# A second norm written chunk by chunk, and the gather that loads its rows as stationaries

## The chip, the cores and the metric

One core of a Trainium2 chip runs the whole step in one launch. The metric is the device time of that launch in microseconds (us): the median of the runs, 1483.82 us before. The engines are TensorE (PE, with its weight loads shown apart as PEld), VectorE (DVE), ScalarE (ACT), GpSimd (POOL) and SyncE (SP), which issues most of the DMAs.

## The reference, cut to what matters

One layer of a streaming encoder on 384 tokens (256 of a prompt, 8 x 16 of samples) with a model width of 1024, all in float32: a projection, a pooling branch and sparse attention, an output projection, and then

```
h2 = rmsnorm(x, norm2_g)                        # x / rms(x) * g, per token
logits = h2 @ w_router + b_router               # 32 experts, the best 4 of each token
for each expert e, on its tokens:
    gu = xe @ w_gate_up[e] + b_gate_up[e]       # 1024 -> 2 x 1024
    a  = min(g, 7) * sigmoid(1.702 g) * (clip(u, -7, 7) + 1)
    y  = a @ w_down[e] + b_down[e]              # 1024 -> 1024
x = x + sum over the 4 experts of gate * y
```

The weights of the 32 experts are 32 x (8 + 4) MB, and each is read once from HBM.

## The kernel before, in words

The tokens are NT = 3 tiles of 128 rows. The width of 1024 is worked on in KC = 8 chunks of 128 for the contraction. Chunk c holds the columns c, c + 8, c + 16, ... (index q * 8 + c), since the weights are loaded with eight neighbouring rows per partition.

**Head.** The projection, attention and the output projection come first. Line 1348 is the output projection, and line 914 adds it to x. The second norm (lines 906 to 909) follows on DVE: `h2[:, t, :]` is x times the reciprocal root times the row `g2row`, three instructions of 1024 elements, one per token tile. PE transposes h2 (lines 1357 and 1361, 24 transposes of 128 x 128) for the router (line 1368). In a transpose h2 is the stationary operand and the identity is the moving one. DVE then works out the selection and the rank of each token in its expert.

**Experts.** The experts go in pairs, two at a time, 64 slots each. DVE writes a 0/1 matrix `pick` (tokens x 128 slots, line 987) for a pair. The gather on PE (line 1404) multiplies it with h2, so that the chosen tokens land transposed in PSUM: 8 chunks times 3 tiles, `h2[:, t, c::KC]` as the stationary and `pick` as the moving operand. A float32 product is two loads and two matmuls in the trace, so a gather is 48 instructions of each kind. ACT (line 672) and DVE (line 993) copy the result to xT. Then come the gate and up products (line 1418, eight units of 1 MB of weights per expert), the transposes back (line 1471), the activation on DVE and ACT, the down products (line 1429, four units per expert), and the rows are added back by a third product (line 1438) and DVE (line 1018).

PE's order is written out by hand: `gather(1)` and the eight gate and up units of expert 0, then 15 turns of a loop, each with two experts and the gather of the next pair between the gate and up units and the down units of its first expert, then a last turn without a gather. So there are 16 gathers, of which 15 are in the loop.

**The weights' queue.** SP issues the expert weights as 384 DMAs of 1 MB in the order in which PE takes them, into 12 slots. The first 12 are loaded during the head. Each later one waits until PE has used the unit 12 places earlier (`unit_used`, line 394), and PE waits for each unit's landing (`slot_wait`, line 1410).

Of the kernel before, what the change touches and what calls it, by code (L numbers as in the profile page):

```python
# [22 lines left out]
ALU = mybir.AluOpType  # L23
# [3 lines left out]
P = 128  # L27
D = 1024
KC = D // P
SEQ, DEC_B, DEC_S, PAST = 256, 8, 16, 128  # L30
NT = (SEQ + DEC_B * DEC_S) // P
# [98 lines left out]
def build(nc, I, O):  # L130
    keep = ExitStack()
    with keep:
        def sem(name):
            return keep.enter_context(nc.semaphore(name))
# [5 lines left out]
        def fixed(name, shape, dt=F32):  # L140
            n = int(np.prod(shape[1:])) * 4
            t = nc.alloc_sbuf_tensor_at(name, shape, dt, offset=cursor[0])
            cursor[0] += (n + 31) // 32 * 32
            return t

        ring = fixed("ring", [P, RING, UCOL])
        x = fixed("x", [P, NT, D])
# [9 lines left out]
        def at(name, kib, shape, dt=F32):  # L157
            off = region + int(kib * 1024)
            assert off + int(np.prod(shape[1:])) * 4 <= nc.sbuf_usable_end, (name, off)
            return nc.alloc_sbuf_tensor_at(name, shape, dt, offset=off)  # L160
# [50 lines left out]
        mix_a = at("mix_a", 92, [P, 512])  # L211
        mixT = at("mixT", 120, [P, KC, TOK])

        h2 = at("h2", 64, [P, NT, D])
        sq2 = at("sq2", 76, [P, D])
        h2T = at("h2T", 114, [P, KC, TOK])
        rt = at("rt", 126, [P, 8, NT * E])
# [17 lines left out]
        g2row = at("g2row", 60, [P, D])  # L235
        eps = small[:, 0:1]
        ssx = small[:, 1:4]
        rsx = small[:, 4:7]
# [8 lines left out]
        bank = [keep.enter_context(nc.psum_tensor(f"bank{i}", [P, 512], F32)) for i in range(8)]  # L247
        scratch = nc.dram_tensor("bias_rows", [H, NREL], F32)

        ident = cst[:, C_ID:C_ID + P]  # L250
        ustrict = cst[:, C_US:C_US + P]

        def bc(t, off, dims, parts=P, p0=0):

            row = int(np.prod(t.shape[1:]))
            return bass.AP(t, off + p0 * row, [[row, parts]] + [list(d) for d in dims])
# [24 lines left out]
        sumsq2, rms2, h2_ready, h2_turned, h2t_ready, route_done = (sem(s) for s in ("sumsq2", "rms2", "h2_ready", "h2_turned", "h2t_ready", "route_done"))  # L281
# [21 lines left out]
        V, A, T, G = nc.vector, nc.scalar, nc.tensor, nc.gpsimd  # L303
# [14 lines left out]
        def half_head(h):  # L318
            return h // 2, 64 * (h % 2)
# [402 lines left out]
        def _(dve):  # L722
            count = [0]

            def step(ins):

                count[0] += 1
                ins.then_inc(vchain, 1)
                dve.wait_ge(vchain, count[0])
# [53 lines left out]
            def ones_like(ap):  # L783
                n = ap.shape[1]
                return bc(small, 95, [(0, n)])
# [110 lines left out]
            for k, m in enumerate(MIXED):  # L896
                t, n = divmod(m, 2)
# [6 lines left out]
            def second_norm(t):  # L904

                dve.wait_ge(rms2, t + 1)
                dve.wait_ge(x1_ready, 2 * (t + 1))
                step(V.reciprocal(rsx[:, t:t + 1], rsx[:, t:t + 1]))
                V.scalar_tensor_tensor(h2[:, t, :], x[:, t, :], rsx[:, t:t + 1], g2row[:], ALU.mult, ALU.mult).then_inc(h2_ready, 1)

            for m in range(2 * NT):
                t, n = divmod(m, 2)
# [3 lines left out]
                if m == 4:  # L916
                    dve.wait_ge(g2_in, 16)
                    second_norm(0)
                    second_norm(1)
            second_norm(2)  # L920
            dve.wait_ge(h2_ready, NT)
            for c in range(1, KC, 2):
# [14 lines left out]
            for t in range(NT):  # L937
                last = V.max(small[:, 8 + 8 * t:16 + 8 * t], lg[:, t * E:(t + 1) * E])
# [7 lines left out]
            for t in range(NT):  # L946
                c = slice(t * E, (t + 1) * E)
                last = V.tensor_tensor_scan(pre[:, c], ones_like(eq[:, c]), eq[:, c], 0.0, ALU.mult, ALU.add)
# [14 lines left out]
            for q in range(MAXPASS):  # L963
                last = V.tensor_scalar(rank_all[:, q, :, :], rt[:, 5, :].rearrange("p (t e) -> p e t", t=NT), -float(q * SLOTS),
                                       None, ALU.add)
# [40 lines left out]
            for u in range(2 * NT):  # L1006
                t, h = divmod(u, 2)
# [59 lines left out]
        def _(pe):  # L1067
# [3 lines left out]
            for c in range(KC):  # L1071
                for t in range(NT):
                    last = T.transpose(bank[c][:, t * P:(t + 1) * P], xn[:, t, c::KC], ident)
# [7 lines left out]
            def turn_twice(b, col, rows):  # L1081

                for r in (0, 64):
                    last = T.matmul(b[r:r + 64, col:col + P], rows, ident, start=True, stop=True)
                return last
# [21 lines left out]
            for b in range(4):  # L1107
                last = turn_twice(bank[7], b * P, ikc[:, b, :])
            last.then_inc(pe_small, 1)
            pe.wait_ge(small_out, 1)  # L1110
            for b in range(4):
                last = turn_twice(bank[6], b * P, ikc[:, 4 + b, :])
# [5 lines left out]
            for t in range(2):  # L1118
                for c in range(2):
                    last = T.transpose(bank[7][:, (2 * t + c) * P:(2 * t + c + 1) * P], zi[:, t, c * P:(c + 1) * P], ident)  # L1120
# [3 lines left out]
            for t in range(2):  # L1124
                last = turn_twice(bank[6], (2 + t) * P, zi[:, t, 256:320])
# [35 lines left out]
            for m in range(5):  # L1161
                if m >= 2:
                    pe.wait_ge(flip_out, m - 1)
                if m < 4:
                    last = T.matmul(bank[6 + m % 2][:, :], flip[:, 0:P], biasR[:, 2 * m:2 * m + 2, :].rearrange("p h k -> p (h k)"),
                                    start=True, stop=True)
                else:
                    last = T.matmul(bank[6][:, 0:PAST + DEC_S], flip[:, P:2 * P], bS0[:], start=True, stop=True)
# [20 lines left out]
            for m in range(8):  # L1189
                if m >= 2:  # L1190
                    pe.wait_ge(turned_out, m - 1)
                for t in range(NT):
                    last = T.transpose(bank[6 + m % 2][:, t * P:(t + 1) * P], zqk[:, t, m * P:(m + 1) * P], ident)
# [32 lines left out]
            for t in range(2):  # L1226
# [5 lines left out]
                for h in range(H):  # L1232
                    c, r = half_head(h)
                    b = bank[h % 2 + 2 * (c // hpb)]
                    col = (c % hpb) * nk
                    last = T.matmul(b[:, col:col + nk], qT[r:r + 64, c, t * P:(t + 1) * P], kT[r:r + 64, c, 0:nk],
                                    start=True, stop=True)
# [4 lines left out]
                for h in range(H):  # L1242
                    c, r = half_head(h)
                    for kc in range(nkc):
                        last = T.matmul(bank[0][r:r + 64, c * P:(c + 1) * P], zv[:, kc, h * HD:(h + 1) * HD],
                                        pT[:, h * nkc + kc, :], start=(kc == 0), stop=(kc == nkc - 1))
# [5 lines left out]
            for r in range(2):  # L1252
                unit_wait(pe, kc_u + r)
                for m in range(4):
                    if r:
                        pe.wait_ge(ks_out, 4)
                    for c in range(PAIRS):
                        last = T.transpose(bank[4 + m][:, c * P:(c + 1) * P],
                                           ring[:, (kc_u + r) % RING, m * 512 + c * P:m * 512 + (c + 1) * P], ident)
# [3 lines left out]
                for m in range(4):  # L1263
# [4 lines left out]
                    for c in range(PAIRS):  # L1268
                        T.matmul(out[:, o:o + P], qblk[:, m, c, :], kTs[:, m, c, :], start=False, stop=False)  # L1269
                        last = T.matmul(out[:, o + P:o + 256], qblk[:, m, c, :], kT[:, c, 2 * P:], start=False,  # L1270
                                        stop=(c == PAIRS - 1))
# [12 lines left out]
            def branch(m, src, u0, b, c):  # L1284

                t, n = divmod(m, 2)
                o = (c % 2) * D + 512 * n
                return T.matmul(bank[b][:, :], src[:, c, t * P:(t + 1) * P], ring[:, (u0 + c // 2) % RING, o:o + 512],  # L1288
                                start=(c == 0), stop=(c == 3))
# [4 lines left out]
            for b in range(DEC_B):  # L1294
                for half in range(2):
                    for c in (2 * half, 2 * half + 1):
# [3 lines left out]
                        last = T.matmul(out, zv[:, 2, c * P:(c + 1) * P], pT[:, 2 * b + 1, 32 * c:32 * c + 32], start=False, stop=True)  # L1300
                    if b >= 2:
                        m, c = dense[2 * (b - 2) + half]
# [16 lines left out]
            for n, m in enumerate(MIXED):  # L1319
# [7 lines left out]
                for c in range(4):  # L1327
                    last = branch(m, attT, wba_u, 2 * (m % 4) + 1, c)
# [4 lines left out]
            for m in range(2 * NT):  # L1333
                t, hf = divmod(m, 2)
                pe.wait_ge(mix_ready, 2 * NT)
                for q in range(4):
                    last = T.transpose(bank[m][:, q * P:(q + 1) * P], mixed[:, t, 4 * hf + q::KC], ident)
# [3 lines left out]
            for m in range(2 * NT):  # L1341
                t, n = divmod(m, 2)
# [3 lines left out]
                for c in range(KC):  # L1346
                    o = (c % 2) * D + 512 * n
                    last = T.matmul(bank[6 + m % 2][:, :], mixT[:, c, t * P:(t + 1) * P],  # L1348
                                    ring[:, (wo_u + c // 2) % RING, o:o + 512], start=(c == 0), stop=(c == KC - 1))
# [4 lines left out]
            pe.wait_ge(h2_ready, 2)  # L1354
            for c in range(6):
                for t in range(2):
                    T.transpose(bank[c][:, t * P:(t + 1) * P], h2[:, t, c::KC], ident)
            pe.wait_ge(h2_ready, NT)
            for c in range(KC):
                for t in range(2 if c < 6 else 0, NT):  # L1360
                    last = T.transpose(bank[c][:, t * P:(t + 1) * P], h2[:, t, c::KC], ident)
                last.then_inc(h2_turned, 1)
            pe.wait_ge(h2t_ready, KC // 2)
            pe.wait_ge(ht_ready_v, KC)
# [1 line left out]
            for t in range(NT):  # L1366
                for c in range(KC):
                    last = T.matmul(bank[0][:, t * E:(t + 1) * E], h2T[:, c, t * P:(t + 1) * P], wr[:, c, :],  # L1368
                                    start=(c == 0), stop=(c == KC - 1))
            last.then_inc(route_done, 1)  # L1370

            for hf in range(2):
# [3 lines left out]
                for c in range(KC):  # L1376
                    last = T.transpose(bank[1][:, c * E:(c + 1) * E], bgn[:, c::KC], cst[0:E, C_ID:C_ID + E])
# [9 lines left out]
            for t in range(NT):  # L1387
                last = T.matmul(bank[0][:, 128:128 + E], ones, sel[:, t * E:(t + 1) * E], start=(t == 0), stop=(t == NT - 1))
# [3 lines left out]
            for t in range(NT):  # L1392
                last = T.transpose(bank[5][0:E, t * P:(t + 1) * P], rt[:, 1, t * E:(t + 1) * E], ident)
# [5 lines left out]
            def gather(pairs):  # L1399

                pe.wait_ge(pick_ready, pairs)
                for c in range(KC):
                    for t in range(NT):
                        last = T.matmul(bank[2 + c // 4][:, (c % 4) * P:(c % 4 + 1) * P], h2[:, t, c::KC],  # L1404
                                        pick[:, t, :, :].rearrange("p a s -> p (a s)"), start=(t == 0), stop=(t == NT - 1))
                last.then_inc(gathered, 1)

# [36 lines left out]
            for u in range(KC):  # L1444
                if u < 2 * NT:

                    t, h = divmod(u, 2)
# [81 lines left out]
```

## Time and profile before

| what | us |
|---|---|
| median of 3 runs | 1483.82 (1481.07 to 1484.92) |
| the profiled execution, its own time | 1482.67 |
| its span, first to last instruction | 1480.8 |
| PE matmul busy in the span | 1409.2 (95%) |
| PE weight loads busy | 677.5 (46%) |
| DVE busy | 425.2 (29%) |
| ACT busy | 189.9 (13%) |

HBM read in the span is 439.27 MB. The page names an operand without its buffer number, so h2 reads as `h`; behind the arrow the moving operand stands first and the stationary second (`bank<-pick,h`). A load and its matmul have the same line. Busy times of PE overlap, since a matmul starts before the one ahead of it has ended: how fast a stretch goes is read from the start of one group to the start of the next.

### The profile page before, as it was taken

What the parts mean: (1) busy time and instruction counts of PE and PEld (TensorE: products, weight loads), DVE (VectorE), ACT (ScalarE), POOL (GpSimd) and SP (SyncE); (2) the same over time, 40 slices, a digit from 0 to 9 for tenths busy, and PEclk for the clock granted to TensorE, in tenths of its full rate; (3) what the DMA queues carried; (4) which work ended last, traced back from release to release, by engine and by line L of the source; (5) the groups of instructions that cost most, each with busy time, mean ns of one, the idle gap of its engine ahead of it and who ended that gap; (6) DMA issues with size and microseconds to landing.
All of it is one profiled execution on the core that took longest, in us unless ns stands there. A gap on an engine that the chain in (4) does not pass through costs nothing.

```text
span 1480.8 us, 15864 instructions
## 1 busy us (share of the span) xinstructions
PE 1409.2 (95%) x6011; PEld 677.5 (46%) x6011; DVE 425.2 (29%) x762; ACT 189.9 (13%) x360; POOL 33.2 (2%) x36
## 2 busy tenths in 40 slices
PE   5999996899989999999999999999999999999996
PEld 3445454664472543535355353544535354353532
DVE  1164013312223222242322324222232322224233
ACT  3121222300110010110101101010110101011000
POOL 4000003000000000000000000000000000000000
PEclk9999997899969999999999999999999999999998
DMA  8221430314429899999999999999999999999991
GB/s 299 94 77 58 145 114 0 121 57 162 165 96 347 322 422 376 380 418 367 423 377 420 376 367 422 372 423 372 390 407 374 424 366 422 375 378 417 374 422 50
DMA packets 73332, 443.14 MB, mean 299 GB/s; under 512 B 7971, under 2 KB 9787, under 8 KB 23646
## 3 DMA queue, kind: packets, MB, share of 16 engines
q1 hardware_dynamic: 68992, 434.94, 72.6%
q10 hardware_dynamic: 3054, 4.90, 1.0%
q0 software_dynamic: 1264, 2.99, 0.7%
q8 instruction: 16, 0.26, 0.1%
q14 instruction: 6, 0.05, 0.0%
HBM read 439.27 MB, written 3.53 MB: 299 GB/s over the span
## 4 chain that ended last, share of the span: by engine, by line
PE 79%; DVE 2%; DMA 1%; ACT 1%; issue 0%; DVEq 0%; SPq 0%; POOL 0%; PEldq 0%
PE bank L1418 31%; PE bank L1429 15%; PE bank L1404 13%; PE bank L1438 7%; PE bank L1288 3%; PE bank L1348 3%; PE bank L1471 2%; PE bank L1484 1%; DMA wpool<-in_w_pool 1%; PE bank L1368 1%; PE bank L1300 1%; PE bank L1299 0%; PE bank L1270 0%; PE bank L1269 0%; DMA ring<-in_w_out 0%; ACT logit L593 0%
## 5 line engine op out<-in xcount | busy, mean ns | idle before, releaser
L1418 PE MATMUL bank<-ring,xT 128*64 128x512 f32 x2048 | 474.9, 600 | 0.0
L1418 PEld LDWEIGHTS bank<-ring,xT 128*64 128x64 f32 x2048 | 132.7, 136 | 284.5 <-issue 280.0
L1429 PE MATMUL bank<-ring,aT 128*64 128x512 f32 x1024 | 226.9, 596 | 0.0
L1404 PEld LDWEIGHTS bank<-pick,h 128*128 128x128 f32 x768 | 184.1, 335 | 15.8 <-issue 12.2
L1404 PE MATMUL bank<-pick,h 128*128 128x128 f32 x768 | 187.1, 405 | 3.2 <-DVE pick L987 3.2
L1018 DVE TENSOR_TENSOR x<-x,bank 128x512 f32<-128x512 f32 x198 | 127.2, 684 | 128.5 <-PE bank L1438 128.5
L1098 PE MATMUL bank<-ring,hT 128*128 128x512 f32 (+1 forms) x384 | 159.1, 574 | 1.0 <-DMA ring<-in_w_in 0.7
L1429 PEld LDWEIGHTS bank<-ring,aT 128*64 128x64 f32 x1024 | 72.4, 137 | 139.9 <-issue 138.1
L1438 PE MATMUL bank<-yS,back 64*128 64x512 f32 x396 | 112.9, 647 | 8.4 <-DVE x L1018 7.6
L1098 PEld LDWEIGHTS bank<-ring,hT 128*128 128x128 f32 x384 | 72.3, 190 | 83.9 <-issue 79.8
L1031 DVE TENSOR_TENSOR gz<-bank,bguT 128x512 f32<-128x512 f32 x64 | 41.2, 686 | 218.9 <-PE bank L1471 218.9
L998 DVE COPY gus<-bank 128x512 f32<-128x512 f32 x32 | 22.1, 692 | 194.9 <-PE bank L1418 194.9
L1438 PEld LDWEIGHTS bank<-yS,back 64*128 64x128 f32 x396 | 30.0, 186 | 88.4 <-DVE x L1018 61.4
L993 DVE COPY xT<-bank 128x512 f32<-128x512 f32 x16 | 11.1, 693 | 174.6 <-PE bank L1404 174.6
L688 ACT ACTIVATE back<-bank 128x384 f32<-128x384 f32 x32 | 15.7, 491 | 343.4 <-PE bank L1484 343.4
L693 ACT ACTIVATE yS<-bank 128x512 f32<-128x512 f32 x32 | 19.1, 597 | 204.2 <-PE bank L1429 204.2
L1471 PEld LDWEIGHTS bank<-cst,gus 128*128 128x128 f32 x256 | 31.1, 194 | 27.0 <-issue 25.2
L1348 PE MATMUL bank<-ring,mixT 128*128 128x512 f32 x96 | 41.4, 593 | 1.1 <-DMA ring<-in_w_out 1.1
L677 ACT ACTIVATE gus<-bank 128x512 f32<-128x512 f32 x32 | 19.1, 598 | 167.2 <-PE bank L1418 167.2
L1471 PE MATMUL bank<-cst,gus 128*128 128x128 f32 x256 | 37.2, 288 | 1.0 <-DVE gus L998 1.0
L672 ACT ACTIVATE xT<-bank 128x512 f32<-128x512 f32 x16 | 9.6, 598 | 179.7 <-PE bank L1404 179.7
L1348 PEld LDWEIGHTS bank<-ring,mixT 128*128 128x128 f32 x96 | 18.2, 190 | 24.0 <-issue 24.0
(247 smaller groups left out, 779.9 us busy)
## 6 DMA issues: line engine op xcount, KB each, us to landing
ring<-in_w_gate_up SPq DMA_DIRECT2D x256, 1024.0 KB, 9.2
ring<-in_w_down SPq DMA_DIRECT2D x128, 1024.0 KB, 9.3
ring<-in_w_in SPq DMA_DIRECT2D x16, 1024.0 KB, 8.0
ring<-in_w_out SPq DMA_DIRECT2D x4, 1024.0 KB, 5.9
ring<-in_cache_k SPq DMA_DIRECT2D x2, 1024.0 KB, 6.8
ring<-in_cache_v SPq DMA_DIRECT2D x2, 1024.0 KB, 6.7
ring<-in_w_branch_pool SPq DMA_DIRECT2D x2, 1024.0 KB, 6.9
ring<-in_w_branch_attn SPq DMA_DIRECT2D x2, 1024.0 KB, 11.3
```

Source lines behind the costliest of these rows:

```text
L677: A.activation(gus[:, 0:512], bank[0][:, :], ACT.Copy).then_inc(gu_out_a, 1)
L998: V.tensor_copy(gus[:, 512:FF], bank[1][:, :]).then_inc(gu_out_v, 1)
L1018: V.tensor_tensor(x[:, t, 512 * h:512 * h + 512], x[:, t, 512 * h:512 * h + 512], bank[6 + h][:, :], ALU.add).then_inc(y_added, 1)
L1031: V.tensor_tensor(gz[:, 4 * b:4 * b + 4, :, :], bank[2 + b][:, :].rearrange("p (c h s) -> p c h s", c=4, h=2), bc(bguT, bias + 4 * b, [(1, ...
L1098: last = T.matmul(bank[3 * (m % 2) + t][:, 0:w], hT[:, c, t * P:(t + 1) * P], ring[:, u % RING, (c % 4) * w:(c % 4 + 1) * w], start=(c == ...
L1288: return T.matmul(bank[b][:, :], src[:, c, t * P:(t + 1) * P], ring[:, (u0 + c // 2) % RING, o:o + 512], start=(c == 0), stop=(c == 3))
L1348: last = T.matmul(bank[6 + m % 2][:, :], mixT[:, c, t * P:(t + 1) * P], ring[:, (wo_u + c // 2) % RING, o:o + 512], start=(c == 0), stop=( ...
L1404: last = T.matmul(bank[2 + c // 4][:, (c % 4) * P:(c % 4 + 1) * P], h2[:, t, c::KC], pick[:, t, :, :].rearrange("p a s -> p (a s)"), start ...
L1418: last = T.matmul(bank[j][64 * r:64 * r + 64, :], xT[:, w, SLOTS * a:SLOTS * a + SLOTS], src[:, FF * r + 512 * j:FF * r + 512 * j + 512], ...
L1429: last = T.matmul(bank[4][64 * r:64 * r + 64, :], aT[:, c, :], src[:, o:o + 512], start=(c == 0), stop=(c == KC - 1))
L1438: last = T.matmul(bank[6 + h][:, :], back[64 * h:64 * h + 64, t, :], yS[64 * h:64 * h + 64, :], start=True, stop=True)
L1471: last = T.transpose(bank[2 + c // 4][:, (c % 4) * P:(c % 4 + 1) * P], gus[:, c::KC], ident)
```

## The change

The tile h2 gets the same bytes in another order. It is now `[128, 3, 8, 128]`: for each token the 128 elements of chunk 0 stand together, then those of chunk 1, and so on. The norm writes it so by reading x and the gain row through a view that steps by 8 elements (32 bytes) within a chunk. The transposes and the gather then take a chunk as 128 neighbouring elements. Number, shape and order of the instructions on all engines are the same as before, as are the waits.

```diff
-        h2 = at("h2", 64, [P, NT, D])
+        h2 = at("h2", 64, [P, NT, KC, P])
...
+        def by_chunk(ap):
+            return ap.rearrange("p (q c) -> p c q", c=KC)
...
-                V.scalar_tensor_tensor(h2[:, t, :], x[:, t, :], rsx[:, t:t + 1], g2row[:], ALU.mult, ALU.mult).then_inc(h2_ready, 1)
+                V.scalar_tensor_tensor(h2[:, t, :, :], by_chunk(x[:, t, :]), rsx[:, t:t + 1], by_chunk(g2row[:]), ALU.mult, ALU.mult).then_inc(h2_ready, 1)
...
-                    T.transpose(bank[c][:, t * P:(t + 1) * P], h2[:, t, c::KC], ident)
+                    T.transpose(bank[c][:, t * P:(t + 1) * P], h2[:, t, c, :], ident)
...
-                    last = T.transpose(bank[c][:, t * P:(t + 1) * P], h2[:, t, c::KC], ident)
+                    last = T.transpose(bank[c][:, t * P:(t + 1) * P], h2[:, t, c, :], ident)
...
-                        last = T.matmul(bank[2 + c // 4][:, (c % 4) * P:(c % 4 + 1) * P], h2[:, t, c::KC],
+                        last = T.matmul(bank[2 + c // 4][:, (c % 4) * P:(c % 4 + 1) * P], h2[:, t, c, :],
                                         pick[:, t, :, :].rearrange("p a s -> p (a s)"), start=(t == 0), stop=(t == NT - 1))
```

## Rows read from the trace of the kernel before

**Rows 1.** The chain that ended last, by line, from the page.
```profile
PE bank L1418 31%; PE bank L1429 15%; PE bank L1404 13%; PE bank L1438 7%; PE bank L1288 3%; PE bank L1348 3%; PE bank L1471 2%; PE bank L1484 1%; DMA wpool<-in_w_pool 1%; PE bank L1368 1%; PE bank L1300 1%; PE bank L1299 0%; PE bank L1270 0%; PE bank L1269 0%; DMA ring<-in_w_out 0%; ACT logit L593 0%
```
**Rows 2.** PE's waits from 442 to 1450 us: total, times, longest.
```profile
PE bank L1471 <- DVE gus L998: 1.0, 1, 1.0
```
**Rows 3.** PE in order of time, two gathers: start, length, line, operands.
```profile
483.41 11.69 PE L1404 MATMUL bank<-pick,h 128*128 128x128 f32 x48
495.03 7.09 PE L1429 MATMUL bank<-ring,aT 128*64 128x512 f32 x32
...
547.39 11.69 PE L1404 MATMUL bank<-pick,h 128*128 128x128 f32 x48
```
**Rows 4.** Weight loads by line and shape: busy us, mean ns, idle before.
```profile
L1404 PEld LDWEIGHTS bank<-pick,h 128*128 128x128 f32 x768 | 184.1, 335 | 15.8 <-issue 12.2 <-DVE pick L987 3.6
...
L1269 PEld LDWEIGHTS bank<-kTs,qblk 128*128 128x128 f32 x64 | 10.3, 192 | 0.4
...
L1258 PEld LDWEIGHTS bank<-cst,ring 128*128 128x128 f32 x32 | 3.5, 141 | 1.4 <-issue 1.4
...
L1361 PEld LDWEIGHTS bank<-cst,h 128*128 128x128 f32 x12 | 1.4, 194 | 2.3 <-DVE h L909 2.3
```
**Rows 5.** PE in order of time, first 16 attention products of lines 1269, 1270.
```profile
255.54 0.38 PE L1269 MATMUL bank<-kTs,qblk 128*128 128x128 f32 x2
...
257.33 0.60 PE L1267 MATMUL bank<-neg,rep 128*128 128x256 f32 x2
```
**Rows 6.** The same view, 16 products of lines 1299 and 1300.
```profile
292.06 0.61 PE L1299 MATMUL bank<-pT,ring 128*128 128x32 f32 x2 [1.96 <-DMA wpool<-in_w_pool]
...
295.47 1.20 PE L1309 MATMUL bank<-ext,wpool 128*128 128x256 f32 x2
```
**Rows 7.** Stretches: us, busy by engine, granted clock, DMA share, GB/s.
```profile
255.50:257.30 1.80, 1.80 (x17) 1.77 (x17) 0.00 (x0) 0.00 (x0) 0.00 (x0) 1.00 0.00 0
292.00:295.40 3.40, 3.34 (x16) 3.37 (x17) 0.00 (x0) 1.70 (x4) 0.00 (x0) 0.50 1.03 410
...
430.60:434.60 4.00, 4.00 (x17) 4.00 (x17) 0.82 (x2) 0.00 (x0) 0.00 (x0) 0.50 0.00 0
434.60:438.60 4.00, 4.00 (x19) 4.00 (x18) 0.00 (x0) 0.00 (x0) 0.00 (x0) 0.85 0.00 0
...
446.00:490.00 44.00, 43.04 (x180) 17.66 (x179) 13.53 (x22) 3.80 (x6) 0.00 (x0) 1.00 0.99 375
490.00:496.00 6.00, 6.00 (x28) 5.31 (x29) 0.69 (x1) 0.60 (x1) 0.00 (x0) 1.00 0.12 51
505.00:552.00 47.00, 47.00 (x211) 17.89 (x208) 16.27 (x28) 5.22 (x9) 0.00 (x0) 1.00 1.01 421
...
1337.00:1384.00 47.00, 47.00 (x211) 18.10 (x207) 16.13 (x27) 4.97 (x9) 0.00 (x0) 1.00 1.01 422
```
**Rows 8.** PE in order of time, the first gather and the first unit.
```profile
430.55 11.75 PE L1404 MATMUL bank<-pick,h 128*128 128x128 f32 x48 [3.16 <-DVE pick L987]
...
443.28 1.94 PE L1418 MATMUL bank<-ring,xT 128*64 128x512 f32 x8
```
**Rows 9.** DVE: the third norm; then two lines' ns, min/median/max, and shapes.
```profile
405.63 1.28 DVE L909 SCALAR_TENSOR_TENSOR h<-x,small,g2row 128x1024 f32<-128x1024 f32 x1
...
L964 DVE TENSOR_SCALAR rank_all<-rt x6: 204/206/217, 426.7 to 427.4; 128x96 f32<-128x96 f32 x6
...
L792 DVE TENSOR_SCALAR neg<-is_gt x3: 226/293/293, 79.3 to 136.7; 128x256 f32<-128x256 f32 x2, 128x128 f32<-128x128 f32 x1
```
**Rows 10.** The page's DMA issues: count, KB each, us to landing.
```profile
ring<-in_w_gate_up SPq DMA_DIRECT2D x256, 1024.0 KB, 9.2
ring<-in_w_down SPq DMA_DIRECT2D x128, 1024.0 KB, 9.3
```
**Rows 11.** PE in order of time, the last turn.
```profile
1449.97 1.16 PE L1471 MATMUL bank<-cst,gus 128*128 128x128 f32 x8
...
1461.22 8.06 PE L1429 MATMUL bank<-ring,aT 128*64 128x512 f32 x32
```

## The prediction

> **What bounds the kernel now.** I read the chain of waits first. PE's expert products hold most of it, and the gather alone (line 1404) 13% [rows 1]. The list of waits says whether the weights are late: from 442 to 1450 us PE waited once, 1.0 us, for DVE, and never for a weight [rows 2]. So the loop runs at PE's pace, and what a gather gives back counts until something else is late. PE in order of time gives the sizes: the gather takes from 483.41 to 495.03, 11.62 us, and the next starts at 547.39, 63.98 us after the first [rows 3]. The stretches show the queue that stands behind PE: in 14 stretches of 47 us, one in each of 14 loop turns, the weights came at 420 to 423 GB/s with a DMA share of 1.01, the first at 421 and the last at 422. Around the end of the second gather the queue idled, 51 GB/s from 490 to 496, because all slots were full [rows 7]. A unit of 1.0486 MB at 422 GB/s is 2.485 us. A loop turn takes 24 of them, 59.6 us, so the weights have only 4.3 us of slack in 63.98.
>
> **The gather in the loop.** 48 instructions in 11.62 us are 242 ns from start to start. Is it the stationary's step? A gather's load lasts 335 ns; that of line 1269, whose stationary is contiguous and whose shape is the same, 192. Line 1361, a transpose of the stepped h2, loads in 194, and line 1258, a transpose of a contiguous tile, in 141 [rows 4]. In both kinds the stepped operand costs more. The first gather is a second witness: its first stretch ran at a granted clock of 0.50, its end at full clock [rows 7], and yet it took 11.7 us like the others [rows 3, 8]. PE's clock does not set its pace; the read of the stationary can.
>
> The pace without the step is read from lines 1269 and 1270: same type, 128 x 128 stationary, 128 moving columns. 16 instructions start from 255.54 to 257.33, 112 ns each, at a granted clock of 1.00 [rows 5, 7]. That makes a gather 48 x 0.112 = 5.4 us, a saving of 6.2 us, and 15 times that is 94. From the other side: if loads hid behind nothing, each at 192 ns, a gather would take 9.2 us and save 2.4. If the pace has another cause, it saves nothing. I take 112, since it is the measured pace of the same shape.
>
> The skill's rule beside these rows: the Trainium skill, "SBUF — State Buffer", section "Door 1: The DMA port swizzle", says that SBUF is read in lines of 16 bytes and that each access that crosses to a new line pays, so that float32 steps for free only up to 4 elements. The step here is 8. The loads of 335 against 192 ns agree.
>
> **The first gather** ran at half clock from 430.55; the clock of 0.85 over 434.6 to 438.6 puts the rise at 435.8. At half clock a contiguous stationary goes at 213 ns: 16 instructions from 292.06 to 295.47, clock 0.50 [rows 6, 7]. If the rise stays where it was, 5.25 us hold 24.6 instructions, and the other 23.4 take 2.6 us: 7.9 against 11.7, so 3.8 us saved. With the clock low to the end it would take 10.2 (1.5 saved), at full clock all through 5.4 (6.3 saved).
>
> **The second norm.** Three instructions of 1.28 us, of which the third stands on the path [rows 9]; the others run beside the output projection. They now read two operands in steps of 32 bytes. Line 964 reads 96 elements in steps of 128 bytes in 206 ns; line 792, the same operation on contiguous data, takes 226 for 128 and 293 for 256 [rows 9]. That is 0.52 ns per element and extrapolates to 209 for 96: no penalty shows, so I take 0. Were a stepped read as dear as in the gather, 242 / 128 = 1.9 ns per element, and the two operands read one after the other, an instruction would take 3.9 us; all three on the path would add 7.8 us. A gain is not excluded, but I see no row for one.
>
> The rule above speaks against this edit: by it the norm pays what the gather is spared. The 206 ns do not show that, and the sum by it stays within the 7.8 us just bounded.
>
> **The transposes** of lines 1357 and 1361 lose some 53 ns of load each, 12 of them on the path [rows 4]. DVE's and ACT's copies follow them one for one and are slower, so I count 0; if all of it showed, 0.6 us.
>
> **What is late next.** PE alone: 94 + 3.8 = 98 us off, a span of 1480.8 - 98 = 1383, and 63.98 - 6.2 = 57.7 us per turn. The weights need 59.6. PE starts the loop with 12 loaded units, falls behind by 1.9 us a turn of that lead, and from about the middle waits for landings. The end by the weights: the first loop unit is released when the first eight products of line 1418 end, 445.2 [rows 8]; 3.8 us earlier now, 441.4. The first 16 units after that took until 490.5 (375 GB/s over 44 us is 16.5 MB, the stretch behind it 0.3 [rows 7]), 45.3 us, because PE releases them slowly there beside the down-bias products. That stays, and the second gather is now over before the slots fill, so the queue does not idle again. There are 256 + 128 units [rows 10], of which 12 are preloaded and 16 just counted; the last four arrive during the last turn's own work of 11.3 us, between 1449.97 and 1461.22 [rows 11], and do not bind. That leaves 384 - 12 - 16 - 4 = 352 units of 2.485 = 874.7 us: 441.4 + 45.3 + 874.7 = 1361.4. PE takes that unit in 1.8 us, and what follows it (from 1449.97 to the span's end) took 30.8: span 1394. This is later than PE's 1383, so it binds. The saving is 87 us, not 98.
>
> The profiled execution took 1482.67, 1.9 us over its span, and the median of the runs is 1.15 above that. 1394 + 3 gives **1397 us**.
>
> **Rivals.**
> Half the gain: the loads are not hidden at 192 ns each, a gather of 9.2 us; 15 x 2.4 + 1.5 = 38 us, 1446. Paces between lie between; at 145 ns the loop is PE's, a gather of 7.0, and the time is 1412. Lines 1269 and 1270 speak against it, since their loads last 192 and still go every 112.
>
> The weights are no bound: PE's 1383 + 3, so 1386. That would need over 436 GB/s (25.17 MB in 57.7 us); no stretch of 47 us shows over 423. The page cited above, in section "SBUF: two separate sides", gives 436 GB/s as the DMA ceiling and 432 as measured; by 432 the time would be 1386 to 1387 too. The traces bear that out little, 422 being steady.
>
> It doesn't do what it says: 242 ns come from another operand; 1484. Against it stand rows 4; `pick` and the PSUM target are contiguous.
>
> Slower: the waits for landings take PE's clock away. The first gather, after 3.16 us without work, ran at a clock of 0.50, where an instruction costs 213 instead of 112 ns [rows 6 to 8]. Each us of PE work then costs nearly one more. It decides when over 6.3 of the 57.7 us in a turn run at half clock; at a fifth of them a turn takes 69.2 us and the time is 1386 + 15 x 11.5 = 1558. For it: PE will wait. Against: 1.9 us of waiting per turn, split over several units, under a us each, and PE is busy 97% of the turn.
>
> **How the numbers follow.** Forecast 0.72, own range 1388 to 1406: the rate of 420 to 423 is ±4, the norm up to +7.8, the first gather ±2.4. No bound by the weights 0.08, half the gain or so 0.13, no effect 0.04, slower 0.03. The range 1382 to 1418 holds the first two and the near part of the third. This kernel's runs differ by some 0.3%, about 4 us, which is what a measurement can tell; by that faster is 0.93, no change 0.04, slower 0.03.
>
> **What would show it.** A gather of 5.4 us in PE's order; loads of line 1404 near 192 ns; from the middle of the loop waits of line 1418 and 1429 for DMA into the ring, with 422 GB/s and no idle stretch; turns of 57.7 us early and 59.6 late; line 909 still at 1.28. I am wrong if a gather stays above 7 us, if the loop's clock leaves 1.00, or if the rate of the weights is another once they bind.

## The result, and the profile after

The changed kernel takes 1407.7 us (median of 4 runs, 1405.8 to 1410.0) against 1482.9 before (by now the median of 4 runs): a ratio of 0.949 with a 95% interval of 0.947 to 0.952. The forecast was 1397, its range 1382 to 1418. The profiled execution took 1405.8 us, with a span of 1404.0.

The new view reads like the old one: the page's chain by line, in which the lines named have moved by four (the gather is line 1408 now, the expert products 1422 and 1433).

```profile
PE bank L1422 27%; PE bank L1433 13%; DMA ring<-in_w_gate_up 9%; PE bank L1408 6%; PE bank L1442 6%; DMA ring<-in_w_down 4%; PE bank L1352 3%; PE bank L1292 3%; PE bank L1475 2%; PE bank L1488 1%; DMA wpool<-in_w_pool 1%; PE bank L1304 1%; PE bank L1372 1%; PE bank L1274 1%; PE bank L1273 1%
```

The gather fell from 13% to 6%, and 13% of the chain are now DMAs of expert weights, which the list before does not have [rows 1]. The list of PE's waits from 442 to 1373 us (total, times, longest) names them, where only the last of these rows stood before [rows 2]:

```profile
PE bank L1433 <- DMA ring<-in_w_down: 6.1, 14, 0.7
PE bank L1422 <- DMA ring<-in_w_gate_up: 1.3, 4, 0.6
PE bank L1475 <- DVE gus L1002: 1.0, 1, 1.0
```

PE in order of time (start, length, line), at two early and two late gathers:

```profile
482.63 5.62 PE L1408 MATMUL bank<-pick,h 128*128 128x128 f32 x48
488.18 7.09 PE L1433 MATMUL bank<-ring,aT 128*64 128x512 f32 x32
...
540.53 5.62 PE L1408 MATMUL bank<-pick,h 128*128 128x128 f32 x48
...
1242.48 5.62 PE L1408 MATMUL bank<-pick,h 128*128 128x128 f32 x48
...
1302.20 5.62 PE L1408 MATMUL bank<-pick,h 128*128 128x128 f32 x48
```

A gather takes 488.18 - 482.63 = 5.55 us in place of 11.62 [rows 3], 116 ns per instruction. The early turn is 57.9 us long, the late one 59.7. All turns from the second gather to the one at 1003.7 take 57.9, the five after it 59.6 to 59.7. The weight loads (busy us, mean ns, idle before), of the gather and of the two groups of transposes of h2:

```profile
L1408 PEld LDWEIGHTS bank<-pick,h 128*128 128x128 f32 x768 | 88.7, 195 | 15.8 <-issue 12.2 <-DVE pick L991 3.6
...
L1365 PEld LDWEIGHTS bank<-cst,h 128*128 128x128 f32 x12 | 2.4, 223 | 3.2 <-DVE h L913 3.2
...
L1361 PEld LDWEIGHTS bank<-cst,h 128*128 128x128 f32 x12 | 1.3, 140 | 0.9 <-issue 0.9
```

The gather's 195 and line 1361's 140 are close to the 192 and 141 ns of the contiguous tiles [rows 4]. Line 1361 here was line 1357 before, with a median load of 193 ns. Line 1361 of [rows 4] is line 1365 now, and it shows no gain, 223 ns for 194. But the granted clock was 0.52 over its 3.5 us and 1.00 before, so these two cannot be compared. The stretches show the weights' queue (columns as in [rows 7]):

```profile
434.10:438.10 4.00, 3.96 (x19) 3.96 (x20) 0.86 (x2) 0.00 (x0) 0.00 (x0) 0.53 0.00 0
...
444.40:490.00 45.60, 44.64 (x213) 17.44 (x213) 14.20 (x23) 4.40 (x7) 0.00 (x0) 1.00 0.97 366
490.00:540.00 50.00, 50.00 (x230) 16.46 (x228) 17.62 (x30) 5.52 (x9) 0.00 (x0) 1.00 0.99 405
540.00:598.00 58.00, 58.00 (x290) 22.59 (x286) 19.00 (x32) 6.71 (x11) 0.00 (x0) 1.00 1.01 422
1200.00:1260.00 60.00, 59.08 (x290) 22.52 (x290) 18.99 (x32) 6.71 (x11) 0.00 (x0) 1.00 1.01 421
444.40:1371.00 926.60, 917.20 (x4469) 349.51 (x4467) 297.98 (x501) 103.10 (x170) 0.00 (x0) 1.00 1.01 418
```

From 540 to 1368 us every stretch of 6 us shows 415 to 429 GB/s; an idle one like that of 51 GB/s before [rows 7] is gone. The units stay in the queue for longer: from issue to landing a gate and up unit now takes 21.3 us in place of 9.2 [rows 10].

```profile
ring<-in_w_gate_up SPq DMA_DIRECT2D x256, 1024.0 KB, 21.3
```

DVE's third norm, and PE's first gather, first unit and last turn, in order of time:

```profile
408.45 2.05 DVE L913 SCALAR_TENSOR_TENSOR h<-x,small,g2row 128x1024 f32<-128x1024 f32 x1
```
```profile
434.14 7.38 PE L1408 MATMUL bank<-pick,h 128*128 128x128 f32 x48 [3.15 <-DVE pick L991]
441.45 1.12 PE L1454 MATMUL bank<-bdn,gT 32*128 32x512 f32 x2
442.50 1.94 PE L1422 MATMUL bank<-ring,xT 128*64 128x512 f32 x8
...
1371.12 1.94 PE L1433 MATMUL bank<-ring,aT 128*64 128x512 f32 x8 [0.54 <-DMA ring<-in_w_down]
1372.99 1.16 PE L1475 MATMUL bank<-cst,gus 128*128 128x128 f32 x8
...
1384.03 8.42 PE L1433 MATMUL bank<-ring,aT 128*64 128x512 f32 x32
```

The norm is dearer, 2.05 us for 1.28 [rows 9]. The first gather takes 7.3 us for 11.7 [rows 8]. The products of line 1433 at 1371.12 wait for their landing, as do those just before them.

### The profile page after: what moved, and what is told of

Read it like the earlier page. It is cut to its first block, busy times and chain, and to the rows that moved or that the text cites. A ratio compares the mean times of both kernels' runs of the same rounds, so it can differ in the third digit from the quotient of the medians.

```text
span 1404.0 us, 15864 instructions
## 1 busy us (share of the span) xinstructions
PE 1321.5 (94%) x6011; PEld 578.8 (41%) x6011; DVE 427.5 (30%) x762; ACT 189.5 (13%) x360; POOL 33.2 (2%) x36
## 4 chain that ended last, share of the span: by engine, by line
PE 65%; DMA 14%; DVE 2%; ACT 1%; issue 1%; DVEq 0%; SPq 0%; POOL 0%; PEldq 0%
PE bank L1422 27%; PE bank L1433 13%; DMA ring<-in_w_gate_up 9%; PE bank L1408 6%; PE bank L1442 6%; DMA ring<-in_w_down 4%; PE bank L1352 3%; PE bank L1292 3%; PE bank L1475 2%; PE bank L1488 1%; DMA wpool<-in_w_pool 1%; PE bank L1304 1%; PE bank L1372 1%; PE bank L1274 1%; PE bank L1273 1%
## 5 line engine op out<-in xcount | busy, mean ns | idle before, releaser
L1433 PE MATMUL bank<-ring,aT 128*64 128x512 f32 x1024 | 230.7, 598 | 6.4 <-DMA ring<-in_w_down 6.1
L1408 PEld LDWEIGHTS bank<-pick,h 128*128 128x128 f32 x768 | 88.7, 195 | 15.8 <-issue 12.2
L1408 PE MATMUL bank<-pick,h 128*128 128x128 f32 x768 | 91.8, 280 | 3.2 <-DVE pick L991 3.2
L829 DVE SCALAR_TENSOR_TENSOR logit<-bank,logit 128x512 f32<-128x512 f32 x6 | 3.8, 683 | 74.4 <-PE bank L1240 74.3
## 6 DMA issues: line engine op xcount, KB each, us to landing
ring<-in_w_gate_up SPq DMA_DIRECT2D x256, 1024.0 KB, 21.3
```

What stands on the lines that cost most here:

```text
L1433: last = T.matmul(bank[4][64 * r:64 * r + 64, :], aT[:, c, :], src[:, o:o + 512], start=(c == 0), stop=(c == KC - 1))
```

## The experiments

Times are medians with the number of runs where there are several; spans are those of the profiled execution.

**1. The gather alone in steps again.**

```diff
-                        last = T.matmul(bank[2 + c // 4][:, (c % 4) * P:(c % 4 + 1) * P], h2[:, t, c, :],
+                        last = T.matmul(bank[2 + c // 4][:, (c % 4) * P:(c % 4 + 1) * P], by_step(t, c, KC),
```
(`by_step(t, off, step)` is the view of the tile's 1024 columns from `off` in steps of `step`.)

> The changed kernel with the norm and the transposes by chunk, but the gather alone reads its stationaries in steps of 8 elements again (it so takes other columns of h2 than the reference). Theory A, the step of the stationary sets the gather's pace: 242 ns per instruction again, 11.6 us per gather, turns of 64.0 us, no wait of PE for a weight in the loop, a time of 1481 to 1488, some 1 us of it the dearer norm. Rival B, the gain came from the transposes or from the new place of the data: the gather stays near 5.6 us and the time near 1408.

Measured: 1485.6 us, span 1483.8. PE in order of time:

```profile
486.34 11.69 PE L1412 MATMUL bank<-pick,h 128*128 128x128 f32 x48
497.96 5.37 PE L1437 MATMUL bank<-ring,aT 128*64 128x512 f32 x24
```

The gather takes 11.62 us again, all loop turns 64.0, and PE waits for no weight. The chunked norm and the contiguous transposes are still there, so the gather's read accounts for the gain, and rival B falls.

**2. Which step costs: chunk c of a gather in steps of c + 1.**

```diff
+                for t in range(NT):
+                    last = T.matmul(bank[2][:, 0 * P:1 * P], by_step(t, 0, 1), ...)
+                for t in range(NT):
+                    last = T.matmul(bank[2][:, 1 * P:2 * P], by_step(t, 0, 2), ...)
...
```

> The changed kernel, but chunk c of a gather reads its stationary in steps of c + 1 elements, 1 to 8, each chunk on a line of its own (so it takes other columns of h2 than the reference). Theory A, the load pays for each line of memory that it touches anew: no more than 112 to 120 ns per instruction at steps 1 and 2, rising to 242 at step 8, with the jump at one step between. Rival B, any step other than 1 costs the whole 242. Rival C, the price grows evenly with the step, some 19 ns per element. The Trainium skill, SBUF - State Buffer, Door 1: The DMA port swizzle, puts the jump between 4 and 5 elements (16 bytes); by it chunks 1 to 4 take 0.67 us each and chunks 5 to 8 1.45 us, 8.5 us for a gather, against 10.9 by rival B.

Measured: 1454.9 us. One gather in order of time, steps 1 to 8 from top to bottom, and the line behind it:

```profile
484.80 0.94 PE L1411 MATMUL bank<-pick,h 128*128 128x128 f32 x6
485.57 0.87 PE L1413 MATMUL bank<-pick,h 128*128 128x128 f32 x6
486.28 1.21 PE L1415 MATMUL bank<-pick,h 128*128 128x128 f32 x6
487.32 1.56 PE L1417 MATMUL bank<-pick,h 128*128 128x128 f32 x6
488.72 1.52 PE L1419 MATMUL bank<-pick,h 128*128 128x128 f32 x6
490.07 1.51 PE L1421 MATMUL bank<-pick,h 128*128 128x128 f32 x6
491.42 1.54 PE L1423 MATMUL bank<-pick,h 128*128 128x128 f32 x6
492.80 1.59 PE L1425 MATMUL bank<-pick,h 128*128 128x128 f32 x6
494.32 6.23 PE L1449 MATMUL bank<-ring,aT 128*64 128x512 f32 x28
```

From start to start, by six: 128, 118, 173, 233, 225, 225, 230 and 253 ns. A step of 2 is free, 3 is half way, and from 4 on the price is nearly flat. Theory A holds in kind, though step 1 took 128 ns for its 112 to 120 and the rise takes two steps and not one. Rivals B and C fall: step 2 costs nothing, and step 4 costs 233 ns where an even growth gives about 170.

The first gather of this run shows what the clock has to do with it. These are its steps 2 to 5; the granted clock was 0.50 up to the start of the last line:

```profile
434.18 1.49 PE L1413 MATMUL bank<-pick,h 128*128 128x128 f32 x6
435.46 1.49 PE L1415 MATMUL bank<-pick,h 128*128 128x128 f32 x6
436.74 1.59 PE L1417 MATMUL bank<-pick,h 128*128 128x128 f32 x6
438.12 1.42 PE L1419 MATMUL bank<-pick,h 128*128 128x128 f32 x6
```

Steps of 2 and 3 go at 213 ns here, the pace that a contiguous stationary showed at half clock with 32 moving columns [rows 6], and a step of 4 at 230. At half clock, then, a step of 4 costs 17 ns per instruction; at full clock it costs over 100.

The Trainium skill, "SBUF — State Buffer", section "Door 1: The DMA port swizzle", names 16-byte lines and two hits per line for full rate. The rows agree with that: a step of 2 leaves two float32 in 16 bytes, a step of 4 one. They contradict the same passage where it lets float32 step by 4 for free; by that a gather would have taken 8.5 us, and it took 494.32 - 484.80 = 9.5.

**3. The norm reads straight and writes in steps.**

```diff
-                V.scalar_tensor_tensor(h2[:, t, :, :], by_chunk(x[:, t, :]), ...
+                V.scalar_tensor_tensor(h2[:, t, :, :].rearrange("p c q -> p q c"), x[:, t, :].rearrange("p (q c) -> p q c", c=KC), ...
```

> The changed kernel, but the norm reads x and the gain row as they stand and writes in steps: each element goes 128 elements (512 bytes) behind the last. The result in h2 is the same. In the changed kernel the norm took 2.05 us where it took 1.28 before. Theory A, the two stepped reads cost the 0.77 us and a stepped write costs nothing: 1.28 us again, and the first gather starts 0.8 us earlier after the end of the last output product. Rival B, any step costs, or a step of 512 bytes costs more: 2.05 us or above. The time moves by at most 3 us either way, so only the trace tells.

Measured: 1407.7 us. The third norm:

```profile
405.75 1.96 DVE L913 SCALAR_TENSOR_TENSOR h<-x,small,g2row 128x1024 f32<-128x1024 f32 x1
```

Theory A falls in its second half: a stepped write costs 0.68 us (1.96 - 1.28) where two stepped reads cost 0.77 (2.05 - 1.28). Of rival B it holds that any step costs; 1.96 is just below its 2.05.

**4. The norm's three tiles in steps of 2, 4 and 8.**

```diff
+                c = (2, 4, 8)[t]
-                V.scalar_tensor_tensor(h2[:, t, :, :], by_chunk(x[:, t, :]), ...
+                V.scalar_tensor_tensor(h2[:, t, :, :]..., by_chunk(x[:, t, :], c), ...
```

> The changed kernel, but the norm of the first token tile reads in steps of 2 elements (8 bytes), that of the second in steps of 4 (16 bytes), and that of the third in steps of 8 as the change has it (so the columns of h2 stand in another order than the reference's in the first two). Theory E, VectorE's read behaves as the stationary's load did, whose pace was that of a contiguous one at a step of 2 and nearly the full price at 4: 1.28, then 2.05, then 2.05 us. Rival F, VectorE pays for any step: 2.05 us in all three. Rival G, it pays only beyond 16 bytes: 1.28, 1.28, 2.05.

Measured, DVE in order of time (1408.5 us):

```profile
399.17 1.29 DVE L914 SCALAR_TENSOR_TENSOR h<-x,small,g2row 128x1024 f32<-128x1024 f32 x1
...
400.56 2.08 DVE L914 SCALAR_TENSOR_TENSOR h<-x,small,g2row 128x1024 f32<-128x1024 f32 x1
...
407.67 2.05 DVE L914 SCALAR_TENSOR_TENSOR h<-x,small,g2row 128x1024 f32<-128x1024 f32 x1
```

Theory E holds within 0.03 us in all three numbers. VectorE's reads are free at a step of 2 and pay in full at 4, as the stationary's load does; a step of 3 was not run here.

**5. Half of each down unit's bytes, in the changed kernel.**

```diff
-                    sp.dma_start(slot_of(DEPTH + k), src).then_inc(slot_in[k % DEPTH], 16)
+                    cols = UCOL if w < KC else UCOL // 2
+                    sp.dma_start(slot_of(DEPTH + k)[:, 0:cols], src[:, 0:cols]).then_inc(slot_in[k % DEPTH], 16)
```

> The changed kernel, but in the loop and the last turn a unit of the down weights loads only half of its columns (the other half of the slot keeps older data). A turn then moves 21.0 MB in place of 25.2, 49.7 us at 422 GB/s, and PE's work is the same. Theory A, from the tenth turn on the weights' queue sets the time: no wait for a landing is left, all turns take 57.9 us, 5 x 1.8 us of the late turns and some 5.7 us of the last turn go, and the span is 1404 - 14.6 = 1389 (with 3 us for the head's clock). Rival C, the late turns are longer for another reason (clock, memory traffic at large): they stay at 59.7 and the span near 1404.

Measured: 1393.6 us, span 1391.8. PE's waits from 442 to 1370:

```profile
PE bank L1444 <- DVE x L1024: 4.9, 2, 3.4
PE bank L1477 <- DVE gus L1004: 1.0, 1, 1.0
```

Two late gathers, PE in order of time:

```profile
1236.67 5.62 PE L1410 MATMUL bank<-pick,h 128*128 128x128 f32 x48
...
1294.57 5.62 PE L1410 MATMUL bank<-pick,h 128*128 128x128 f32 x48
```

No wait for a landing is left, and all 14 gather-to-gather times of the loop are 57.9 us. The first unit started 1.3 us later than in the changed kernel (443.84 against 442.50), and the span is 12.2 us shorter; from the first unit on it is 13.5 us, where 14.6 were expected. So the waits for the weights' queue make the late turns longer. Of rival C, the clock was 1.00 in early and late turns alike. The halving cuts the traffic as well, but the traffic is no cause either: in the changed kernel it was 422 GB/s in an early turn of 57.9 us and 421 in a late one of 59.7.

**6. The same halving in the kernel before.**

> The kernel before, but in the loop and the last turn a unit of the down weights loads only half of its columns. Theory A, the weights were no bound there, and what PE does goes no faster beside less traffic: turns of 64.0 us, a span of 1478 to 1484. Rival D, the traffic itself slows PE or the loads of its stationaries: turns under 63.5 us and a span under 1475.

Measured: 1483.9 us, turns of 63.97 to 63.98. The stretch of one turn (columns as above):

```profile
484.60:548.60 64.00, 64.00 (x289) 28.67 (x287) 19.01 (x32) 6.71 (x11) 0.00 (x0) 1.00 0.86 318
```

At 318 GB/s in place of some 393 (24 units in 64.0 us) PE's turn is as long as before: this traffic does not slow it, and rival D falls.

**7. The bias products moved to the last turn, and the changed kernel again.** The six products with the down bias leave the first eight units; they come behind the last four gate and up units and the first two down units of the last turn.

```diff
-                    T.matmul(bank[6 + u % 2][:, :], gT[:, t, :], bdn[:, 512 * h:512 * h + 512],
-                             start=True, stop=True).then_inc(bd_done, 1)
...
+                        if final and a == 0 and w >= 4:
+                            bias_rows(n, w - 4)
```

> The changed kernel as it is, timed in five rounds on the chip on which the next one is timed. Theory A, the loop goes from 57.9 us per turn to 59.7 when the weights bind, as in the first trace: ratio to before 0.947 to 0.952. What differs between runs of it is the head, where the granted clock falls for some us at other places each time: the last product of the output projection should start up to 4 us earlier or later.

> The changed kernel, but the six products with the down bias, which stand between the first eight weight units (6.3 us of PE), move to the last turn, where PE waits some 0.5 us for each of its last units. Not one product fewer. Theory A, the weights' queue sets the end: PE gets 6.3 us further ahead early, the units are released and loaded sooner, and in the last turn the products fill waits that are there anyway; part of the 6.3 us comes out, some 3.5 us by a count with the releases, so a span some 3 to 5 us under that of the changed kernel, a ratio of the two of about 0.9975. Rival C, PE's own work sets the end: the work is only moved, and the time stays within 1 us.

DVE's six additions of these products move with them.

Measured, five runs each on the same chip: the changed kernel 1408.2 us (1404.9 to 1410.2; 0.949 of before, 0.947 to 0.952), the other 1404.4 (1402.8 to 1408.1; 0.947, 0.944 to 0.949). The medians differ by a ratio of 0.9974, as expected, but the runs and the intervals overlap, so the times do not tell the two apart. The changed kernel's second profile goes from turns of 57.9 to 59.7 us again, and its transposes behind the output projection start at 405.41, against 406.14 in the first, within the 4 us expected.

The spans miss what was expected, 3 to 5 us less: 1403.8 with the late bias, 1404.0 and 1403.1 in the two profiles of the changed kernel. The traces say where it went. Late bias, PE in order of time, and a stretch behind the last transposes (columns as in [rows 7]):

```profile
434.84 8.52 PE L1416 MATMUL bank<-pick,h 128*128 128x128 f32 x48 [3.15 <-DVE pick L991]
444.35 13.96 PE L1430 MATMUL bank<-ring,xT 128*64 128x512 f32 x64 [0.99 <-DVE xT L997]
...
1371.84 1.16 PE L1485 MATMUL bank<-cst,gus 128*128 128x128 f32 x8
...
1377.00:1381.00 4.00, 2.08 (x4) 0.50 (x4) 2.22 (x5) 0.00 (x0) 0.00 (x0) 0.50 0.00 0
```

From the end of the first gather to the last transposes it takes 928.5 us, against 931.5 in the changed kernel (1372.99 - 441.52), with the six products in both. 3.0 us came out (2.7 against the second profile), and rival C's exact balance does not fit. The first unit now waits 0.99 us for DVE's xT; that is within the 928.5, and the first bias product's 1.05 us stood there before. But this run's first gather ended 1.8 us later than in the first profile of the changed kernel, and the tail behind the last transposes took 32.0 us for 31.0: the granted clock was 0.50 from 1377 to 1381 us, where the changed kernel had 0.82 from 1378 to 1381. That leaves the 0.2 us between the spans of 1403.8 and 1404.0. Whether the whole launch is faster stays open.

## Why the prediction held, and where it was off

**The gather.** The pace of 112 ns per instruction was read from another line and came out as 116. 15 times (11.62 - 5.55) is 91 us, where 94 stood in the sum. That the gather did not follow PE's clock was the right witness: experiments 1 and 2 show the read of the stationary as the cause. Of the signs named, the gathers of the loop are under 7 us. The first one took 7.3, under the 7.9 of the sum.

**The weights.** The bound named as next is the one found, from the gather at 1003.7 us on, somewhat past the middle of the loop. PE's turns are 57.9 (57.7 forecast), the queue's 59.7 (59.6 forecast). Experiment 5 puts the price of this bound at 13.5 us from the first unit on (12.2 of the span, as its head was later); the forecast was 1394 - 1383 = 11.

**The 10 us between the spans of 1394 and 1404.0.** The median of 1407.7 is within the wide range but 1.7 us above the prediction's own one, 1388 to 1406. By the sum's own terms (the median stands 3.7 us above its profile's span, where 3 was added):

- The weights' term was 6.7 us short. From the first release at 444.4 to the unit at 1371.1 it took 926.7 us, and 45.3 + 874.7 = 920 were forecast. "The queue does not idle again" held, but full rate began a turn late: 405 GB/s over the 50 us from 490 cost 2 us. The rate behind it was 421 to 422, worth another 1 us or so on 352 units. And 418 GB/s over 926.6 us are 369.4 units, where 368 were counted. The stretch behind agrees: from 1371.1 to 1384 us 3.1 MB came, 2.9 units, where four were still to come by the sum. So bytes of later units had landed before the one that PE waited for, 1.1 to 1.4 units or some 3 us. That the deeper queue is the reason is argued and not shown.
- The head was 2.8 us later with no changed instruction on its path. The last output product starts at 405.39 against 402.57, and this lag stood before the first norm ran at 399.95: of the projection's matmuls 61 came after 379.6 us, before the change 54 after 379.8. In ten profiles, of kernels with the same work on PE up to there, it starts between 401.9 and 405.4. This spread was not in the range's terms.
- From the second group of transposes (line 1365, line 1361 before) to the first gather it took 23.58 us, as before. That is luck: the transposes lost 0.9 us at a granted clock of 0.52 (1.00 before), and the router's products behind them gained 0.9 at 0.72 (0.64 before). In six of the ten profiles this stretch took 25.6 to 26.0 us, with 10.4 us for the router's products in place of 7.4 to 8.3.
- The norm cost 0.77 us on the path, and 0 was taken. The prediction names the case that the norm pays and sets it aside for line 964. The step that failed is this reading: a scalar operation on 96 elements in steps of 128 bytes showed no penalty, and that did not carry over to a norm of 1024 elements and two stepped operands. Experiment 4 says from which step it pays, not why line 964 does not.
- The first gather took 7.3 us, forecast 7.9, which gave 0.6 back. Over 434.1 to 438.1 the clock was 0.53, so it rose at about 437.9 and not at 435.8, but the gather had started 3.6 us later. In the trace of experiment 3 the same gather took 8.4 us, at 0.50 over its first 4.0; the 0.6 is luck.
- The rest, 0.2 us, is the tail: 31.0 us from the last transposes to the end, 30.8 before.

**The rivals.** Half the gain fell with the pace, "doesn't do what it says" with experiment 1. That the weights are no bound fell: the rate stayed at 421 to 422 GB/s. The clock stayed at 1.00 in the stretches with waits, which are at most 0.7 us each; the rival on the slower side did not occur.

## What to carry to other kernels

Compare a stationary's load time with that of a contiguous one of the same shape before counting columns: at steps of 4 to 8 float32, a 128 x 128 product with 128 moving columns took 225 to 253 ns in place of 116 at full clock, and at half clock a step of 4 cost 17 ns. A layout change that is paid once, where the tile is written (0.8 us here), can spare every later read of it (16 gathers of 6 us). Before trusting the whole sum, work out the second bound per turn; here it took 12 to 14 us back, and where a slot queue gives a lead the new bound shows only once the lead is used up.

## What the runs showed of the hardware that was not expected

A float32 stationary read in steps of 4 to 8 elements goes at 225 to 253 ns per instruction at full clock, nearly whatever the step, and a step of 2 at the contiguous pace. Before the change a gather took 11.7 us with its first 4 us at half clock and 11.6 at full clock. At half clock, steps of 2 and 3 went at 213 ns and one of 4 at 230. VectorE's norm of 1024 elements takes 1.29 us in steps of 2, 2.08 in steps of 4 and 2.05 in steps of 8, and 1.96 when the write is stepped in place of the reads.
